# Normalised tiles made ahead and kept in HBM as bf16, and weights cast during attention: one decoder layer on eight cores

## What is computed

```python
x = x + 0.5 * swiglu(rmsnorm(x, ffn1_norm), ffn1_w1, ffn1_w3, ffn1_w2)     # 2048 -> 5632 -> 2048
h = rmsnorm(x, mix_norm)
proj = h @ w_in                         # fox q,k,v (8 heads), moba q,k,v (4), memory q (4), forget gates
o = concatenate([fox_attention, moba_attention, memory_attention])         # 16 heads of 128
x = x + o @ w_out
x = x + 0.5 * swiglu(rmsnorm(x, ffn2_norm), ffn2_w1, ffn2_w3, ffn2_w2)
```

## Time and profile before

| | |
|---|---|
| time, median of 3 runs | 4957.62 us (4951.34 to 4967.99) |
| the profiled execution's own time | 4961.24 us |
| its span (slowest core; the eight: 4929.4 to 4959.7) | 4959.7 us |
| PE busy | 4550.5 us, 92% of the span |
| DVE busy | 3233.8 us, 65% |
| ACT busy | 1554.6 us, 31% |
| POOL busy | 381.6 us, 8% |
| HBM read and written | 839.04 MB and 155.36 MB |

### The profile page before, as it was taken

How to read it: one execution, slowest core, us unless ns; L and a number is a source line. 1 busy time by engine, 2 the same in 40 slices (tenths; PEclk the granted TensorE clock), 3 DMA queues, 4 the chain that set the end, 5 groups by cost and what they waited for, 6 DMA issues and landing times.

```text
span 4959.7 us, 66466 instructions; the slowest of 8 cores (4929.4 to 4959.7 us)
## 1 busy us (share of the span) xinstructions
PE 4550.5 (92%) x20296; PEld 1964.0 (40%) x20708; DVE 3233.8 (65%) x5396; ACT 1554.6 (31%) x2696; POOL 381.6 (8%) x525
## 2 busy tenths in 40 slices
PE   3998998999998988889979999889999899999998
PEld 1443443434443433344433333334444344444444
DVE  4765675766776766755544666566777577777765
ACT  2322211132121223556556775223121121212121
POOL 3000000000000000000002321000000000000000
PEclk9999999999999999999999999999999999999999
DMA  4688599676958466423431115896949968585845
GB/s 119 101 173 184 125 209 193 171 174 137 189 99 181 87 197 166 119 56 82 89 103 39 40 52 116 184 187 133 221 87 201 200 162 169 102 204 93 188 94 128
DMA packets 189279, 688.39 MB, mean 139 GB/s; under 512 B 21440, under 2 KB 42368, under 8 KB 138880
## 3 DMA queue, kind: packets, MB, share of 16 engines
q0 software_dynamic: 53136, 377.51, 43.6%
q1 hardware_dynamic: 135792, 306.60, 19.7%
HBM read 839.04 MB, written 155.36 MB: 200 GB/s over the span
## 4 chain that ended last, share of the span: by engine, by line
PE 70%; DMA 13%; DVE 7%; issue 5%; ACT 5%; SPq 0%; POOL 0%; DVEq 0%; ACTq 0%; POOLq 0%
PE ps L371 69%; DMA wraw_46<-wu 2%; DMA out<-xst_59 2%; DMA xst_59<-xr 1%; DMA wraw_45<-wu 1%; DVE acd_131 L346 1%; DMA wraw_45<-wo 1%; DMA out<-yst_58 1%; DMA xst_59<-out 1%; DVE wcmb_47 L346 1%; ACT hrb_91 L368 1%; DMA xst_60<-out 1%; ACT hrb_90 L368 1%; DVE XA L346 1%; DVE t_c_53 L346 1%
## 5 line engine op out<-in xcount | busy, mean ns | idle before, releaser
L371 PE MATMUL ps<-XA,wcmb_47 128*128 128x512 bf16 x3998 | 914.7, 383 | 42.1 <-DVE t_c_53 L346 33.3
L371 PE MATMUL ps<-XA,wcmb_48 128*128 128x512 bf16 x3998 | 904.0, 380 | 26.4 <-DVE t_c_53 L346 15.0
L346 DVE TENSOR_TENSOR wcmb_47<-wraw_45 128x1024 bf16<-128x1024 bf16 (+1 forms) x790 | 505.7, 672 | 244.3 <-DMA wraw_45<-wu 161.9
L371 PEld LDWEIGHTS ps<-XA,wcmb_47 128*128 128x128 bf16 x4080 | 398.0, 99 | 530.3 <-issue 69.5
L346 DVE TENSOR_TENSOR wcmb_48<-wraw_46 128x1024 bf16<-128x1024 bf16 (+1 forms) x790 | 505.5, 672 | 153.4 <-DMA wraw_46<-wu 57.5
L371 PEld LDWEIGHTS ps<-XA,wcmb_48 128*128 128x128 bf16 x4080 | 396.1, 98 | 505.5 <-issue 39.8
L371 PE MATMUL ps<-XB,wcmb_48 128*128 128x512 bf16 x2276 | 521.9, 383 | 45.6 <-DVE yst_58 L346 26.6
L371 PE MATMUL ps<-XB,wcmb_47 128*128 128x512 bf16 x2278 | 519.9, 382 | 31.1 <-ACT t_e_50 L363 11.2
L371 PE MATMUL ps<-XA,wraw_45 128*128 128x512 bf16 x1600 | 386.4, 388 | 53.0 <-DVE XA L346 50.3
L346 DVE TENSOR_TENSOR t_c_54<-ps,t_e_50 128x512 f32<-128x512 f32 x296 | 204.0, 689 | 353.1 <-PE ps L371 338.9
L363 ACT COPY t_e_49<-ps 128x512 f32<-128x512 f32 x328 | 191.4, 584 | 729.1 <-PE ps L371 532.6
(11 more groups left out here) (419 smaller groups left out, 4823.7 us busy)
## 6 DMA issues: line engine op xcount, KB each, us to landing
wraw_45<-wu POOLq DMA_DIRECT2D x88, 1024.0 KB, 9.9
wraw_46<-wu POOLq DMA_DIRECT2D x88, 1024.0 KB, 9.6
xst_59<-out SPq DMA_DIRECT2D x24, 1024.0 KB, 8.5
xst_60<-out SPq DMA_DIRECT2D x24, 1024.0 KB, 10.4
out<-yst_57 SPq DMA_DIRECT2D x88, 256.0 KB, 11.7
out<-yst_58 SPq DMA_DIRECT2D x88, 256.0 KB, 16.4
out<-xst_59 SPq DMA_DIRECT2D x72, 256.0 KB, 18.5
out<-xst_60 SPq DMA_DIRECT2D x72, 256.0 KB, 18.1
```

The lines of the kernel that those rows point to most:

```text
L346: return op(eng, lambda e: e.tensor_tensor(out=o_, in0=a, in1=b, op=alu), R=[a, b], W=[o_])
L371: return op("pe", lambda e: e.matmul(o_, l, r, start=start, stop=stop, skip_group_check=skip), R=[l, r], W=[o_])
```

## The change

Four things at once, and an order that follows from them.

- **Tiles ahead.** In the third up phase of `ffn(0,0)`, `ffn(0,1)` and `ffn(1,0)`, `xstash` loads x in chunks, does the four `scalar_tensor_tensor` into a buffer `hb` and stores it to HBM (`Hs`, 0.5 MB per chunk). In the down phase after it `xfetch` loads the four bf16 tiles (two of them straight into `XA`, two into `bt`) and does only `x_comb`.
- **Adding on DVE.** The buffers `xst` are free in those down phases, so all of them use `dquads_sum` with four buffers; `dquads_acc` is gone. The second half of `outproj` uses `dquads_mix`: two of four tiles by load, DVE and store, two by an adding transfer.
- **Casts during attention.** `conv` no longer goes through SBUF: 16 transfers from HBM to HBM on POOL's queue, one or two at the start of a head, cast `w_out` (`wob`) and the second step's third down block (`wdb`). The first step's third down block is read as f32. The first two loads of `outproj` are issued before attention and stay f32.
- **Startup.** POOL does no arithmetic; DVE squares one of four parts and makes all tiles, in pairs of chunks; the first weight load waits for chunk 6 of x, not for chunk 4.
- `xchunks` loads chunk c in step c and uses it in step c+1, nine steps; the projection's first list has nine quads (a pair of fox keys is moved into it) and is not lagged any more. The scratch for 1/rms (`lnr`) lies in `rb[1]`.

```diff
-        def conv(f):
-            def g(i):
-                dma("pool", cvb[i % 2][:, :], wd[f][2][i], "cvl%d" % (i % 2), R=[])
-                dma("sp", wdb[f][i], cvb[i % 2][:, :], "cvs%d" % (i % 2), W=[("wd", f, i)])
-            return [lambda i=i: g(i) for i in range(8)]
+        def conv():
+            def g(o_, i_, tag, n):
+                dma("pool", o_, i_, "cv%d" % (n % 4), R=[], W=[tag])
+            l = [(wob[i], wo[i], ("wo", i)) for i in range(8)]
+            l += [(wdb[i], wd[1][2][i], ("wd", i)) for i in range(8)]
+            return [lambda a=a, n=n: g(*a, n) for n, a in enumerate(l)]
...
-                    if c == 0:
-                        xst_load(src, tag, tp, 0)
-                    if c < 7:
-                        xst_load(src, tag, tp, c + 1)
-                    use(c, xst[c % 2])
+                    if c < 8:
+                        xst_load(src, tag, tp, c)
+                    if c:
+                        use(c - 1, xst[(c - 1) % 2])
                 return g
-            return [f(c) for c in range(8)]
+            return [f(c) for c in range(9)]
...
+        hb = [sb("hb%d" % i, [128, 4, 512], BF16, (164 + 4 * i) * KB) for i in range(2)]
+        bt = [sb("bt%d" % i, [128, 2, 512], BF16, (200 - 2 * i) * KB) for i in range(2)]
+
+        def xstash(src, tag, tp, ni):
+            def use(c, x):
...
+                for o_, i, g in ((0, 0, g0), (1, 3, ng1), (2, 1, g0), (3, 2, g1)):
+                    stt(h[:, o_, :], x[:, i, :], g, rb[i % 2][:, :], ALU.mult, ALU.mult)
+                dma("sp", Hs[tp, c], flat(h), "hs%d" % (c % 2), W=[("H", tp, c)])
+            return xchunks(src, tag, tp, use)
+
+        def xfetch(X, tp):
+            def load(c):
+                dma("sp", X[:, 1:5:3, c, :], Hs[tp, c, :, 0:1024].rearrange("p (a b) -> p a b", a=2), "hx%d" % (c % 2), R=[("H", tp, c)],
+                    W=[X[:, 1, c, :], X[:, 4, c, :]])
+                dma("sp", flat(bt[c % 2]), Hs[tp, c, :, 1024:2048], "hy%d" % (c % 2), R=[("H", tp, c)])
...
+                    if k == 0:
+                        load(0)
+                    else:
+                        comb(k - 1)
+                    if k < 7:
+                        load(k + 1)
+                    else:
+                        comb(7)
...
-                        ft[f, tp, b, dp] = add(wdb[f][dp], nb, [("wd", f, dp)]) if b == 2 else add(wd[f][b][dp], nb)
+                        ft[f, tp, b, dp] = add(wdb[dp], nb, [("wd", dp)]) if f and b == 2 else add(wd[f][b][dp], nb)
...
-            w_load(0, R=[xs0[4][:, 0, 0:1]])
+            w_load(0, R=[xs0[6][:, 0, 0:1]])
...
-                    actf(q, xs0[c][:, i, :], AF.Square)
+                    if i == 3:
+                        tt(q, xs0[c][:, i, :], xs0[c][:, i, :], ALU.mult)
+                    else:
+                        actf(q, xs0[c][:, i, :], AF.Square)
...
-                for i, k in ((1, c), (2, 8 + c)):
-                    ts(xs0[c][:, i, :], xs0[c][:, i, :], gT[:, k:k + 1], ALU.mult, "pool")
...
+            for c in range(0, 8, 2):
+                for k in (c, c + 1):
+                    half(k, 3, X[:, 4, k, :], ngT[:, 8 + k:9 + k], 1)
+                    half(k, 1, X[:, 5, k, :], gT[:, k:k + 1], 1)
+                tt(X[:, 2, c:c + 2, :], X[:, 5, c:c + 2, :], X[:, 4, c:c + 2, :], ALU.add)
...
-                tt(X[:, 5, c, :], xs0[c][:, 1, :], rb[1][:, :], ALU.mult, "pool")
...
-                if b < 2:
-                    dquads_sum(tl, XB, tp, xr if f == 0 and b == 0 else out, yst + xst, False)
-                elif stats:
-                    dquads_sum(tl, XB, tp, out, yst, True)
-                else:
-                    dquads_acc(tl, XB, tp)
+                dquads_sum(tl, XB, tp, xr if f == 0 and b == 0 else out, yst + xst, stats and b == 2)
...
+                def acc(i, dp=dp, y=y):
+                    def g(v):
+                        tt(y[:, i, :], y[:, i, :], v, ALU.add)
+                        dma("sp", out[tp, dp, :, i * 512:(i + 1) * 512], y[:, i, :], "ys%d%d" % (dp % 2, i), W=[rt(tp, dp)[i]])
+                        if dp < 7:
+                            yload(dp + 1, i)
+                    return g
+                quad(tl[dp], X, y[:, 3, :], y[:, 0, :], acc(1), acc(2), noop1, noop1)
...
-            bg.extend(lagged(xbuild(XB, out, "R", 1, 1)))
+            bg.extend(xbuild(XB, out, "R", 1, 1))
...
+                for _ in range(2 if hi_ % 4 == 1 else 1):
+                    if cv and hi_ >= 3:
+                        cv.pop(0)()
...
-        ffn(0, 0, sched((0, 1, membg()), (14, 1, xstats(xr, "X", 1)), (29, 1, conv(0))), xbuild(XA, xr, "X", 1, 0), False)
+        ffn(0, 0, sched((0, 1, membg()), (14, 1, xstats(xr, "X", 1)), (30, 1, xstash(xr, "X", 1, 0))), xfetch(XA, 1), False)
...
-        ffn(1, 0, sched((1, 1, xstats(out, "R", 1)), (29, 1, conv(1))), xbuild(XA, out, "R", 1, 2), False)
+        ffn(1, 0, sched((1, 1, xstats(out, "R", 1)), (30, 1, xstash(out, "R", 1, 2))), xfetch(XA, 1), False)
```

More of the change, by code:

```diff
@@ L265, in build @@
     MRs = dscr("MRs", [4, 8, 1024], BF16)
-    wdb = [dscr("wdb%d" % f, [8, 128, 4096], BF16) for f in range(2)]
+    wob = dscr("wob", [8, 128, 4096], BF16)
+    wdb = dscr("wdb", [8, 128, 4096], BF16)
+    Hs = dscr("Hs", [2, 8, 128, 2048], BF16)
     cs3 = dscr("cs3", [3, 8, S], BF16)
@@ L472, in stat_mm @@
             mm(ps[7][32 * th:32 * th + 32, :], onesD, q, first, last, skip=True)
[L474 removed]
+        lnr = rb[1][0:64, :]
         def stats_finish():
@@ L568, in build @@
         ts(ngT[:, :], gT[:, :], -1.0, ALU.mult)
-        A_P = list(range(8))
-        B_P = list(range(8, NP))
-        A1_P = [6, 7, 0, 1, 2, 3, 4, 5]
+        A_P = list(range(9))
+        B_P = list(range(9, NP))
+        A1_P = [6, 7, 8, 0, 1, 2, 3, 4, 5]
         ft = {}
@@ L579, in build @@
                 pt_a1 = [add(wp[p], 8) for p in A1_P]
-                ot = [[add(wo[dp], 8) for dp in range(8)] for _ in range(2)]
+                ot = [[add(wo[dp], 8) if h == 0 and dp < 2 else add(wob[dp], 8, [("wo", dp)]) for dp in range(8)] for h in range(2)]
             for tp in range(2):
@@ L606, in startup, with half @@
             actf(lx, lx, AF.Exp, scale=-0.5)
+            for i in (1, 0):
+                mm(ps[5 + i][:, :], cf[0:64, 192 + 128 * i:320 + 128 * i], lx, True, True)
+                (acopy if i == 0 else vcopy)(rb[i][:, :], ps[5 + i][:, :])
+            X = XA
+            def half(c, i, o_, g, r):
+                stt(o_, xs0[c][:, i, :], g, rb[r][:, :], ALU.mult, ALU.mult)
+            for c in range(0, 8, 2):
[3 more added lines that the diff above has]
+                tt(X[:, 2, c:c + 2, :], X[:, 5, c:c + 2, :], X[:, 4, c:c + 2, :], ALU.add)
+            for c in range(0, 8, 2):
+                for k in (c, c + 1):
+                    half(k, 0, X[:, 1, k, :], gT[:, k:k + 1], 0)
+                    half(k, 2, X[:, 6, k, :], gT[:, 8 + k:9 + k], 0)
+                tt(X[:, 3, c:c + 2, :], X[:, 6, c:c + 2, :], X[:, 1, c:c + 2, :], ALU.subtract)
             for p in w_prep(0):
                 p()
[L609 to L615, removed]
-                tt(X[:, 5, c, :], xs0[c][:, 1, :], rb[1][:, :], ALU.mult, "pool")
[L617 to L621, removed]
             for o_, a, b, alu in ((0, 1, 4, ALU.subtract), (5, 1, 5, ALU.add), (6, 6, 4, ALU.subtract)):
@@ L1107, in attention @@
             nxt = first.pop(12)
+            cv = conv()
             for hi_, h in enumerate(horder):
@@ L1131, in build @@
         startup()
-        ffn(0, 0, sched((0, 1, membg()), (14, 1, xstats(xr, "X", 1)), (29, 1, conv(0))), xbuild(XA, xr, "X", 1, 0), False)
-        ffn(0, 1, sched((1, 1, xstats(out, "R", 0))), xbuild(XA, out, "R", 0, 1), True)
+        ffn(0, 0, sched((0, 1, membg()), (14, 1, xstats(xr, "X", 1)), (30, 1, xstash(xr, "X", 1, 0))), xfetch(XA, 1), False)
+        ffn(0, 1, sched((1, 1, xstats(out, "R", 0)), (30, 1, xstash(out, "R", 0, 1))), xfetch(XA, 0), True)
         projection()
```

37 lines of the change are left out of this document (23 added, 14 removed).

## The result

The changed kernel takes 4831.97 us at the median (4805.61 to 4839.81), the kernel before 4954.48 in the same comparison. The ratio on record, 0.9736 with a 95% interval of 0.970 to 0.9772, is that of the means, with a fifth execution of 4821.32 us among those after (the medians give 0.9753). At the medians 122 us are won where 183 were forecast: inside the range of 4722 to 4838, near its slow end, and outside the forecast's own range of 4735 to 4812. The profiled execution, the quickest of its four, took 4805.61 us. (Many later executions ran with the cores of a die at a lower clock; ratios and times leave them out, and of the two profiles that fell in one, the first edit to the statistics is read on the other die's cores and the five edits together not at all.)

The account below looks back on a forecast made before the run. PE was busy 92% of the span, so time could be won only where it waits or runs below its clock. The terms sum to -183 us, from the median of 4957.6 to 4774, range 4722 to 4838.

Parts of the forecast that it names:

- Start: Startup through the first quad: without POOL's arithmetic it ends at 86 in place of 120.0 us, -34.
- `conv` out of the up phases: Third up phases of `ffn(0,0)` and `ffn(1,0)`: less DMA work, the stash's products fit on DVE; -26 and -21 us.
- `projection`: First eight quads of `projection`: a quad of lead and one chunk per step remove both waits, -20 us.
- casts in attention: Sixteen casts on idle DMA engines, each under 1 us of POOL at a head's start: +2 us.
- -7: Third down phase of `ffn(0,0)`: 101 us of DMA work against 97 of PE, 104 in place of 111.4 us.
- -24: Second half of `outproj`: 106 us of DMA work plus a wait for the last chunk, 114 in place of 138.5 us.
- my own sign of being wrong: The forecast counts as wrong if, among other signs, the second half of `outproj` stays above 125 us.
- `ffn(0,1)`: Third down phase: statistics no longer wait behind four products on DVE, 147.5 becomes 113 us, -34.5.
- The stall in the second up phase: First quad of `ffn(0,0)`'s second up phase: x is used one quad later, 7 us of stall stay, -13 us.
- 4830 of the third: Rival on attention: casts only move, each of 16 costing 3.5 us as in a `conv` quad, 56 in all; chance 0.05.
- 4822 of the second: Rival on the stash quads: DVE becomes their bound, 2 us over in each of 24 quads, 48; chance 0.17.
- the fourth: Rival on the fetches: they come late and DVE stops, 11 us in each of 24 quads, 5038 us; chance 0.03.

Follow-up runs that it names:

- the first edit to the statistics: Changed kernel with x for the statistics used two quads after its load, the next load wrongly between second and third square; second up phase 212 to 219 us.
- the five edits together: Changed kernel with later casts, later statistics, three fetch buffers, earlier chunks in `outproj`, and `ffn(0,0)` casting its third down block to bf16: 4805.28 and 4811.10 us.

## Why the prediction was right, and where its sizes were off

- **Direction and mechanism.** Start, `conv` out of the up phases, `projection`, the tail and `ffn(1,0)`'s down phase came within about 3 us of their terms, except for the third up phase of `ffn(1,0)`, 5.5 us better. For these the cause rests on the waits that are gone from the traces; no run puts one of these parts back by itself.
- **The step that failed most: casts in attention.** "Each takes POOL under 1 us at a head's start" took a place in POOL's list for a time. In the four memory heads POOL has no other work, so nothing holds the first two casts back, and they run at the end of `projection`. +2 was +18: about 12 of the 18 are these two casts, which later casts win back, and the rest is the slow head on more cores. The other fourteen cost nothing that shows.
- **Full phases mis-sized.** I added DMA prices from light stretches: 101 us for the third down phase of `ffn(0,0)` and 106 for the second half of `outproj`. The shares after give 115.3 x 0.97 = 112 and 125.4 x 0.95 = 119, some 12% more, and both phases follow those. -7 was +2, -24 was -7.5. For the second my own sign of being wrong, above 125, came true (125.6, and 130 to 135 in the later runs that leave it alone). The Trainium skill ("DMA: Bandwidth & Descriptors", Specifications) gives a limit of about 358 GB/s of HBM per core, by which the first of them would have hidden behind PE; it was not reached. The phase took 115.3 us at 220 GB/s counted, which with its eight weight loads at their f32 size is an estimated 293 GB/s.
- **The last chunk.** I charged 2 us at the end of `ffn(0,1)`'s phase, where it has a single quad of lead, and 6 to 8 in `outproj`, where it has none. The last quads took 24.6 us (against 13.8) and 31.8 (against 12.1) on the slowest core.
- **`ffn(0,1)`: the time right by two causes, one named.** On the slowest core 14 us came from the first quad and 18 from quads two to seven, less 7 given back at the end. I put the whole term down to the order on DVE, which the run with the products back bears out for quads two to seven. The first quad was late by a chunk loaded in the quad that used it, the fault that I named for `projection` alone; that its 14 us stood in my sum was luck.
- **The stall in the second up phase.** It moved by one quad, but on seven cores that quad takes 22 to 25 us and not 12, so about 10 to 12.5 us of it stay where I left 7.
- **Rivals.** The result lies 2 us from the 4830 of the third and 10 from the 4822 of the second, yet by the way of neither. The casts cost attention about 12 us, not 56, and the stash quads run at 12.2, though doubling their products shows that it was a near thing. That several terms which fell short add up to those times is chance. Late fetches, the fourth, came true in the last quads alone.

## What to carry to other kernels

Where in an engine's list a transfer stands tells when it is issued only if the instructions ahead of it wait for something; look at what holds the queue there. A sum of DMA prices taken where the engines are half idle came out some 12% low in two phases in which they are full. And a prefetch ring must be judged by its last chunk, which often has less lead than the others.

## What the runs showed that was not expected

- In some heads of attention the clock stood at 1.2 GHz for 20.5 us, 8 us lost, on six cores after and two before, with PE as busy as on a core that kept 2.4 GHz.
- Taking away 18 us of DMA work (110 to 92) in one phase won 18.7 us of its 115.4. The DMA share alone does not tell such a phase: at 0.97 it took 113 to 115 us, but with smaller weight loads it ran at PE's pace at 0.95, 96.7 us, as that of `ffn(1,0)` did at 0.94 and a steady stretch at 1.02.
- DVE had next to no room left at a busy share of 0.90: 3.0 us more work per quad cost 3.4 us.
